# The second half's norm moved into the first FFN, decode norms cut in two, and whole cache copies on GpSimd's queue, in a decoder layer on eight cores

## The reference

```python
x = x + 0.5 * swiglu(rmsnorm(x, norm_ffn1), ffn1_w_gate, ffn1_w_up, ffn1_w_down)
h = rmsnorm(x, norm_mix)
z = h @ w_in                     # pool input u (512) | 3 head groups x (q, k, v) x 4 heads x 64 | 2 gates (1024 each)
pool = pool_mix(u_ext, pos, w_pool_grp, pool_scale)      # trailing means over 2, 4, 8, 16 rows
attn = ...                       # dilated windows (128,1), (512,4), (2048,16), rotary q/k, merged by denominators
merged = sigmoid(gate_pool) * (pool @ w_pool_br) + sigmoid(gate_attn) * (attn @ w_attn_br)
x = x + merged @ w_o
x = x + 0.5 * swiglu(rmsnorm(x, norm_ffn2), ffn2_w_gate, ffn2_w_up, ffn2_w_down)
y = rmsnorm(x, norm_final)
```

## Time and profile before

| | us |
|---|---|
| median of 3 runs (3095.58 to 3347.91) | 3097.86 |
| the profiled execution | 3097.86 |
| its span on the slowest core (core 3) | 3096.8 |
| spans of the eight cores | 3076.6 to 3096.8 |
| TensorE busy, share of the span | 91% |
| mean granted TensorE clock, core 3 | 0.968 |

### The profile page before, as it was taken

One profiled execution on the slowest core, in us unless ns is written; L12 is line 12 of the kernel. 1 busy time (PEld: TensorE's weight loads), 2 busy tenths in 40 slices (PEclk: granted clock), 3 DMA queues, 4 the chain that ended last, 5 costly groups with the idle time before them and its releaser, 6 DMA issues.

```text
span 3096.8 us, 47383 instructions; the slowest of 8 cores (3076.6 to 3096.8 us)
## 1 busy us (share of the span) xinstructions
PE 2832.2 (91%) x15857; PEld 1365.0 (44%) x15857; DVE 1221.3 (39%) x1881; ACT 909.6 (29%) x1946; POOL 408.6 (13%) x741
## 2 busy tenths in 40 slices
PE   3999668799989998889999999889999999789998
PEld 2445234444444444444444444444444444444443
DVE  4223555532242245443234225453224225544223
ACT  2112334321141136442123126542114115543112
POOL 1001000010020015310001005230002003520000
PEclk9999879999999999999999999999999999899999
DMA  7756636477573234424346334324326223423222
GB/s 172 150 118 147 161 99 167 125 174 177 104 235 135 91 115 134 130 91 141 102 131 219 102 109 146 114 91 162 108 92 228 81 75 108 134 98 121 90 73 85
DMA packets 119335, 397.59 MB, mean 128 GB/s; under 512 B 15243, under 2 KB 30507, under 8 KB 118135
## 3 DMA queue, kind: packets, MB, share of 16 engines
q1 hardware_dynamic: 105147, 346.01, 33.2%
q0 software_dynamic: 13952, 48.55, 9.9%
HBM read 363.78 MB, written 101.39 MB: 150 GB/s over the span
## 4 chain that ended last, share of the span: by engine, by line
PE 79%; DMA 6%; ACT 4%; DVE 4%; issue 4%; POOL 2%; SPq 0%; ACTq 0%; DVEq 0%; POOLq 0%
PE ps L269 77%; DMA x_45<-x 1%; PE ps L279 1%; PE ps L579 1%; DMA v2scr<-vst_81 1%; DMA w_65<-wt 1%; DMA w_63<-wscr 0%; ACT qz_56 L912 0%; ACT poolT L1252 0%; DMA w_65<-wscr 0%; SPq L149 0%; ACT qz_57 L912 0%; POOL qkb_98 L896 0%; DMA kvp<-kf_103 0%; ACT gt_0_141 L1154 0%
## 5 line engine op out<-in xcount | busy, mean ns | idle before, releaser
L567 POOL TENSOR_SCALAR stat<-stat 128x1 f32<-128x1 f32 x128 | 35.0, 273 | 1716.9 <-ACT junk L565 1707.1
L830 ACT ACTIVATE st_110<-ps 128x512 f32<-128x512 f32 x88 | 52.5, 596 | 624.6 <-PE ps L269 624.6
L269 PE MATMUL ps<-hT_48,w_65 128*128 128x512 bf16 x592 | 146.1, 391 | 5.0 <-ACT qz_58 L912 3.6
L833 DVE TENSOR_TENSOR act_109<-st_112,ps 128x512 bf16<-128x512 f32 x79 | 54.3, 688 | 224.6 <-PE ps L269 224.6
L833 DVE TENSOR_TENSOR act_108<-st_110,ps 128x512 bf16<-128x512 f32 x79 | 54.3, 688 | 224.1 <-PE ps L269 208.3
L269 PE MATMUL ps<-hT_48,w_64 128*128 128x512 bf16 x576 | 138.3, 384 | 2.7 <-ACT qz_58 L912 2.6
L833 DVE TENSOR_TENSOR act_108<-st_111,ps 128x512 bf16<-128x512 f32 x79 | 54.3, 688 | 219.1 <-PE ps L269 219.1
L833 DVE TENSOR_TENSOR act_109<-st_113,ps 128x512 bf16<-128x512 f32 x79 | 54.3, 688 | 218.8 <-PE ps L269 218.8
L269 PE MATMUL ps<-hT_48,w_63 128*128 128x512 bf16 x560 | 136.8, 388 | 2.3 <-ACT qz_58 L912 1.5
L269 PE MATMUL ps<-hT_49,w_65 128*128 128x512 bf16 x560 | 132.3, 379 | 2.2 <-DMA w_65<-wscr 2.2
L269 PE MATMUL ps<-hT_49,w_64 128*128 128x512 bf16 x560 | 132.3, 379 | 0.6 <-DMA w_64<-wscr 0.6
(11 more groups left out here) (496 smaller groups left out, 5476.8 us busy)
## 6 DMA issues: line engine op xcount, KB each, us to landing
w_63<-wscr SPq DMA_DIRECT2D x59, 512.0 KB, 4.4
w_69<-wscr SPq DMA_DIRECT2D x59, 512.0 KB, 3.9
w_64<-wscr SPq DMA_DIRECT2D x58, 512.0 KB, 4.4
w_65<-wscr SPq DMA_DIRECT2D x58, 512.0 KB, 4.1
w_66<-wscr SPq DMA_DIRECT2D x51, 512.0 KB, 4.8
w_68<-wscr SPq DMA_DIRECT2D x51, 512.0 KB, 5.0
w_67<-wscr SPq DMA_DIRECT2D x44, 512.0 KB, 4.5
kvs<-c SPq DMA_DIRECT2D x32, 512.0 KB
```

What stands on the lines that cost most here:

```text
L269: self.pe.op(lambda o=o, l=l, r=r, kw=kw: self.nc.tensor.matmul(o, l, r, **kw), reads=rds, writes=[self.psr[bank]] if i == 0 else (), inc= ...
L567: pool.op(lambda: nc.gpsimd.tensor_scalar(st[:, 1:2], st[:, 0:1], 1.0, EPS, op0=ALU.mult, op1=ALU.add), reads=r, writes=r)
L830: act.op(lambda: nc.scalar.activation(out=st[:, :], in_=ps[bg][:, :], func=AF.Silu), reads=[psr[bg]], writes=st.r)
L833: dve.op(lambda: nc.vector.tensor_tensor(out=actb[h][:, jl, :], in0=st[:, :], in1=ps[bu][:, :], op=ALU.mult), reads=st.r + [psr[bu]], writ ...
```

## The change

Three things.

*The start.* SP issues half 0's four blocks, `gain_59`, then half 1's four blocks; POOL issues `cbf` and two weight tiles. Half 0's four blocks are normed, then come loads of the decode rows (already transposed by the host, [128, 32]), their gains and the identity, two more tiles, and `ffn(0)`. Half 1's norm, the other three slots, the decode rows' norm, the constants, the second gain and the rotary tables get due times of 0 to 14 us inside it. The clearing of buffers becomes 16 smaller jobs (`K.chores`), one behind each group of matmul pairs from the fourth pair of tiles on. In pair 0 `s_up` stands behind half 1's groups.

*The decode norms.* `s_norm` does its first two steps at once and puts the rest 2 us later; `s_out` puts its transposes another 2 us later.

*The copies.* 12 whole copies (4 x 4.19 MB, 4 x 1.05 MB, 4 x 0.26 MB) and the small pool copy, on POOL's queue: in pairs 1 to 3 two behind `ffn(0)`, three behind the mixer.

```diff
+        for b in range(4):
+            load_x(0, 0, b, sp)
         load_gain(0, sp)
+        pool.dma(cbf[:], cbf_d[:, :], ds_cbf, writes=cbf.r)
         if not dry:
-            w_issue(len(plan))
+            w_issue(2)
...
-        def s_norm(gi, f32out=None):
+        def s_norm(gi, f32out=None, then=None):
...
+            def rest():
+                b = K.bank()
+                K.mm(b, [(ps[b][:, 0:4], onesf[:, :], s_st[:, 0:4], ())], reads=s_st.r + onesf.r)
...
+                if then:
+                    then()
+            K.later(2.0, rest)
...
-                        if ride and h == 0:
+                        if ride and h == 1:
                             s_up(wg, wu, cs, jl)
                         K.pump()
                     if h == 1:
                         wdone(*held.pop(jp))
-                        if not K.pass0:
-                            copies(1)
+                    if K.chores and jp > 2:
+                        K.chores.pop(0)()
...
-                    for r0 in range(1, Lg, 256):
...
+                    nel = (Lg - 1) * 512
+                    a = 16 if nel % 16 == 0 else 1
+                    src = cache_d[g][bb, 1:Lg, :, :].rearrange("r t f -> (r t f)").rearrange("(a c) -> a c", a=a)
...
-                    sp.dma(dst, src, ds_misc)
+                    pool.dma(dst, src, ds_misc)
...
+        for b in range(4):
+            norm_blk(0, b, 0, d1=0.0, d2=0.0)
         K.flush()
...
+            w_issue(4)
+        for b in range(4):
+            K.later(1.5 * b, lambda b=b: norm_blk(1, b, 0, d1=1.0, d2=1.5))
+        K.later(8.0, lambda: dry or w_issue(len(plan)))
+        if do_sample:
+            K.later(9.0, s_load)
+        K.later(10.0, load_consts)
+        K.later(12.0, lambda: load_gain(1, sp))
+        clear_buffers()
...
             ffn(0, LAG if pr else 1, lambda h, b: norm_blk(h, b, 1))
+            copies(2 if pr else 0)
             load_gain(2, sp)
             mixer(pr, A, B, lambda h, b: norm_blk(h, b, 2, d1=4.0 if h == 0 else 3.0, d2=8.0 if h == 0 else 4.5))
             load_gain(3, sp)
+            copies(3 if pr else 0)
```

More of the change, by code:

```diff
@@ L230, in __init__ @@
         self.marks = []
+        self.chores = []
     def dram_in(self, name, shape):
@@ L452, in build_once @@
         ds_cp = K.dsem("ds_cp")
+        ds_cbf = K.dsem("ds_cbf")
+        ds_id = K.dsem("ds_id")
         ds_x = Rot([K.dsem("ds_x%d" % i) for i in range(8)])
@@ L526, in load_x @@
             eng.dma(dst, x_d[s, r0:r0 + 128, :], ds_x.next(), writes=res)
[L528 to L536, removed]
         gain_cur = {}
@@ L549, in build_once, with load_consts, clear_buffers @@
         dve.op(lambda: nc.vector.memset(mhalf[:], -0.5), writes=mhalf.r)
[L550 to L556, removed]
+        def load_consts():
+            cload(sp, rcnt[:], rcnt_d[:, :, :], rcnt, ds_c)
+            cload(sp, pscale[:], pscale_d.rearrange("(c p) -> p c", p=128), pscale, ds_c, allow_slow_non_contiguous=True)
+            cload(pool, wgrp[:], wgrp_d.rearrange("g c d -> c g d"), wgrp, ds_cp)
+            for buf, dsm in cres:
+                buf.r[0].w = (dsm.sem, dsm.total)
+        def clear_buffers():
+            jobs = [(vst.items[0][:, 64:128], vst.items[0].r), (vst.items[0][:, 256:320], vst.items[0].r),
+                    (vst.items[1][:, 64:128], vst.items[1].r), (vst.items[1][:, 256:320], vst.items[1].r)]
+            jobs += [(v_[:, :, :].rearrange("p n (a c) -> p (n a) c", a=2)[:, :, 64:128], v_.r) for v_ in (V0, V1)]
+            jobs += [(V2[:, 8 * i:8 * i + 8, :], V2.r) for i in range(2)]
+            jobs = [(ap, rs, 1.0) for ap, rs in jobs]
+            jobs += [(q_[:, p], q_.r, 0.0) for q_ in qz for p in range(2)] + [(kT2[:, p], kT2.r, 0.0) for p in range(2)]
+            for ap, rs, val in jobs:
+                K.chores.append(lambda ap=ap, rs=rs, val=val: dve.op(lambda: nc.vector.memset(ap, val), writes=rs))
         K.stat_i = 0
@@ L618, in s_norm @@
                                                    axis=mybir.AxisListType.X, op=ALU.add), reads=s_tmp.r, writes=s_st.r)
[L619 to L628, removed]
+            def rest():
+                b = K.bank()
+                K.mm(b, [(ps[b][:, 0:4], onesf[:, :], s_st[:, 0:4], ())], reads=s_st.r + onesf.r)
+                dve.op(lambda: nc.vector.tensor_scalar(s_st[:, 4:8], ps[b][:, 0:4], EPS, None, op0=ALU.add), reads=[psr[b]], writes=s_st.r)
+                pool.op(lambda: nc.gpsimd.tensor_tensor(out=s_st[:, 8:12], in0=s_st[:, 4:8], in1=mhalf[:, :].broadcast_to([128, 4]), op=ALU.pow),
+                        reads=s_st.r + mhalf.r, writes=s_st.r)
+                dve.op(lambda: nc.vector.tensor_tensor(out=v(s_tmp), in0=v(xTs), in1=s_st[:, 8:12].unsqueeze(1).broadcast_to([128, 8, NS]),
+                                                       op=ALU.mult), reads=xTs.r + s_st.r, writes=s_tmp.r)
+                o = hTs if f32out is None else f32out
+                dve.op(lambda: nc.vector.tensor_tensor(out=v(o), in0=v(s_tmp), in1=gainf[:, gi, :].unsqueeze(2).broadcast_to([128, 8, NS]),
+                                                       op=ALU.mult), reads=s_tmp.r + gainf.r, writes=o.r)
+                if then:
+                    then()
+            K.later(2.0, rest)
         def tposes(items, reads):
@@ L795, in s_out, with rest @@
         def s_out():
[L796 to L800, removed]
+            def rest():
+                for hf in range(2):
+                    b = tposes([(c * 128, s_y[:, (4 * hf + c) * NS:(4 * hf + c + 1) * NS], identf[:, :]) for c in range(4)], s_y.r)
+                    acopy(s_row[:, 0:512], ps[b][0:NS, :], [psr[b]], s_row.r)
+                    sp.dma(ys_d[:, hf * 512:(hf + 1) * 512], s_row[:, 0:512], ds_s.next(), reads=s_row.r)
+            s_norm(3, f32out=s_y, then=lambda: K.later(2.0, rest))
         def ffn(f, lag, after_block, part_hook=None):
@@ L1400, in build_once @@
                 for bb in range(NS):
-                    for r0 in range(1, Lg, 256):
[L1402 to L1407, removed]
+                    nel = (Lg - 1) * 512
+                    a = 16 if nel % 16 == 0 else 1
+                    src = cache_d[g][bb, 1:Lg, :, :].rearrange("r t f -> (r t f)").rearrange("(a c) -> a c", a=a)
+                    dst = kvs_d[g][bb, 0:Lg - 1, :, :].rearrange("r t f -> (r t f)").rearrange("(a c) -> a c", a=a)
+                    pend_copy.append((dst, src))
             pend_copy.append((pools_d[:, 0:14, :], spool_d[:, 1:15, :]))
@@ L1413, in copies @@
                     dst, src = pend_copy.pop(0)
-                    sp.dma(dst, src, ds_misc)
-        for h in range(2):
-            for b in range(4):
-                norm_blk(h, b, 0, d1=0.0, d2=0.0)
+                    pool.dma(dst, src, ds_misc)
+        for b in range(4):
+            norm_blk(0, b, 0, d1=0.0, d2=0.0)
         K.flush()
         if do_sample:
-            s_load()
+            sp.dma(xTs[:, :], xs_d[:, :], ds_s.next(), writes=xTs.r)
+            sp.dma(gainf[:, :, :], gainf_d[:, :, :], ds_s.next(), writes=gainf.r)
+        sp.dma(identf[:], ident_d[:, :], ds_id, writes=identf.r)
+        if not dry:
+            w_issue(4)
[7 more added lines that the diff above has]
+        clear_buffers()
         for pr in range(npair):
@@ L1435, in build_once @@
                 K.later(4.0, lambda: norm_blk(1, 3, 0, stage=stg[3]))
-            sp.dma(ropet[:], rope_d[:, 4 * t0:4 * t0 + 8, :, :], ds_rope, writes=ropet.r)
+            K.later(0.0 if pr else 14.0, lambda t0=t0: sp.dma(ropet[:], rope_d[:, 4 * t0:4 * t0 + 8, :, :], ds_rope, writes=ropet.r))
             ffn(0, LAG if pr else 1, lambda h, b: norm_blk(h, b, 1))
+            copies(2 if pr else 0)
             load_gain(2, sp)
```

10 lines of the change are left out of this document (2 added, 8 removed).

## The result

The changed kernel took 3166.9 us at the median; against the kernel before its time is 1.0228 (1.0205 to 1.0251): slower by 2.3%, above the range of 3066 to 3148.

What follows compares the result with a forecast made beforehand. TensorE, busy 91% of the span, was taken as the bound, with stops at the start and decode norms. Gains of -30.9 us and copy costs of +48 on 3097.9 gave 3115 us, range 3066 to 3148.

Steps and rivals of the forecast that it cites:

- The start: Up to the first FFN: gain at 21, first matmul at 28.3 instead of 56.06, net -21 us (-17 to -25).
- The give-back inside it: Inside the first FFN: half 1's transposes, waits, a copy and decode work return 6.8 us of the 27.8 gained.
- half the start: Rival: the first FFN waits for half 1's rows or tiles and keeps only 10 of 21 us; 3126 us, chance 0.10.
- The decode norms: At s_out the stop shrinks from 21.3 to 12.7 us, -8.6 (-4 to -11); at the first norm -1.3.
- the second norm's saving: At the second decode norm (2.97 us at 648.90): taken as 0, since TensorE waits for w_68 13 us later.
- the whole front: Start and decode norms together: -21, -8.6 and -1.3, sum -30.9 us.
- The copies: On POOL's ring: +31 in pair 1's mixer, +12 behind it, +4 and +1 in pairs 2 and 3; +48 us.
- With the neighbour 7.6 us ahead ... 33.7 us. I take that: Pair 1's mixer: two copies (8.38 MB) at 199 GB/s, the last 3.2 MB at 422, hold the store; +31 us.
- the bound for contention all along: Pair 1's mixer: two copies against a neighbour throughout, at 199 GB/s, last 42.1 us; +40 us.
- the bound for a start at once: Pair 1's second FFN: copies starting right after POOL's step would also catch w_64, needed at 1423.69; +19 us.
- the first rival: Short turns: POOL's long rows are cut into small packets, copies mostly hide, costing +12 us; 3079 us, chance 0.27.
- The contended rival: All four copy places: neighbouring cores copy together at 199 GB/s; +40, +20, +10, +3, 3140 us, chance 0.17.

Runs made afterwards that it cites:

- the first experiment: The changed kernel with cache copies put back as before (44 pieces of 512 KB on SP's queue): 0.9944 of the kernel before, median 3076.4 us.
- short rows: The changed kernel with each copy cut into two of every second row of about 8 KB, same queue and places: 1.0236 against the kernel before.

## Why the prediction was wrong, point by point

*The start* (-21): right. The gain arrived near 20, the first matmul came at 27.7 (28.3 forecast), and 21.2 us were there at the end of the first FFN. The give-back inside it was 5.6 (6.8), and the rival *half the start* fell. What the prediction left out is that pair 0's mixer and second FFN take part of it again, 21.2 down to 17.5 in the mean (4.8 to 25.5 on the single cores). No single wait accounts for that. Two that grew are those on tiles cast from `wt`, 5.3 instead of 2.0 us in the mean, and on VectorE's copy `vf_104`, which were not there before: 5.2 us on core 4, 0.9 to 1.1 on five cores, none on two.

*The decode norms* (-8.6 at `s_out`): right, 9.3 in the mean (-17.5 to -26.8), 12.5 us of stop against 12.7 worked out. That the second norm's saving goes to `w_68` was right as well: that wait is 7.0, where it was 1.21. For the whole front the forecast was -30.9; it stood at -25.4 at pair 1's mixer and at -24.1 at the end of the first experiment, whose time gives 18.

*The copies* (+48): this is the step that failed, in size. In the mean over the cores the sum missed by 50 us, of which 43 are the copies' (91 for 48) and 7 the front's. The place, the store caught behind them, ScalarE's wait and TensorE's stop were as told; the prices were not. "With the neighbour 7.6 us ahead ... 33.7 us. I take that" gave +31; the copies took 44 to 49 us on the eight cores, from the first of their packets to the last, 172 to 189 GB/s, and the mixer lost 45. Even the bound for contention all along was 42. Both rates of the sum were too high, 422 GB/s alone (a piece's 304 over its DMA share of 0.72) and 199 beside a neighbour. Core 6, the first, moved its first copy in 17.8 us (235 GB/s) while SP's own tiles moved beside it, and its second in 27.0 (155 GB/s) once core 7 had begun; on the cores that start late it was the other way round, 27 to 28 us and then 18 to 21. So two neighbours, their first packets 10 to 13 us apart, took the same time whichever led. (Each core's times count from its own start; that the late cores speed up when the early ones end, at 1154 to 1160, says that the starts are close.)

In the second FFN the prediction took +12, with `w_64` safe, since SP would have moved 30 packets an engine by the time the copies start; that price was 34. On the four early cores (1, 2, 5, 6) the tile was the right one and the price too low: `w_63` was waited for 23.0 to 29.9 us, since the three copies took 53 to 60 us from the first issue to the last landing instead of 43.5 (4.7 + 38.8). On the four late cores `w_64` was not safe. On core 4, from 1430 to 1440, SP had moved 357 packets, 22 an engine, and `w_64` is whole with 24; between 1440 and 1475 it moved 85 packets of 4 KB beside 93 of POOL's of 65.5 KB, of which one took some 6 us. So the last few packets of `w_64` (not the same number on each engine) came in turns of 6 us: in effect the bound for a start at once (+19), with `w_63` (8.4) on top. The Trainium skill says in "DMA: Bandwidth & Descriptors", section "Queues, rings and completion order", that an engine goes round its rings a packet at a time; the 85 to 93 agree. The 4096 bytes that the Trainium skill gives there, in section "SWDGE vs HWDGE vs iDMA", and on which the first rival stood, do not hold for these copies: they went in packets of 65,504 bytes. Packets of 8 KB did not save the slowest core's time either.

The contended rival (3140, chance 0.17) named contention, which is nearest to what was seen; with +45, +34, +8 and +2 in place of 40, 20, 10 and 3, and a front of 24, it would have been 3163. Its reason, stalls that pull the cores' starts together, did not come true: neighbours' first stores were 8 to 11 us apart at the mixer, and 5 to 8 before the change.

What stays open: why the copies' rate falls, since no run copied on some of the cores only; why the start alone keeps less of its gain than the start with the put-off norms; and why, with short rows, the one of two neighbours that comes later waits longer for its first store.

## What to carry to other kernels

A large copy between two places in HBM is priced by its bytes at the rate that it gets while the other cores copy too (here 172 to 189 GB/s a core), if anything that the next few microseconds need is queued beside it; ask first where the queue is empty, then how the copy is shaped. A DMA without a wait, on the queue of an engine that idles, starts when that engine reaches it, not where the code put it: give it a wait on the work beside which it belongs. Here the changed front with the old copies, or with whole copies that wait for the sixth tile pair, takes some 0.5% less than the kernel before (0.9944 and 0.9947), small but clear of the noise.

## What the runs showed that was not expected

Cutting packets from 65.5 KB to 8 KB brought the first of four stores in 16.7 us on core 5 but not the fourth: with stores that wait for each other, a fair share per packet is no help there. And copies of 4.19 MB one at a time, in the middle of FFNs, landed 15.4 to 17.7 us after their issue on core 4, while of the two queued at the mixer's start the first landed after 34.1 and the second after 50.8. All cores issued theirs within some 17 us of each other in both kernels.
